# Seven block products in the last up-projection of a streaming encoder, and its start and end in column groups

## What is computed

```python
def rmsnorm(x, gain):
    return x * lax.rsqrt(jnp.mean(x * x, axis=-1, keepdims=True) + EPS) * gain

def conv_ffn(h, hist, w_up, w_conv, b_conv, w_down):      # h: (1, t, 1024), w_up: (1024, 2*2816)
    a, gate = jnp.split(h @ w_up, 2, axis=-1)
    ext = jnp.concatenate([hist, a], axis=1)
    conv = b_conv
    for j in range(3):
        conv = conv + ext[:, j:j + t] * w_conv[j]
    return (jax.nn.silu(conv) * gate) @ w_down, ext[:, t:]
...
    xp = xp + h                       # after both layers: y = rmsnorm(x, final_norm)
```

## Time and profile before

| | |
|---|---|
| median of 3 runs | 4039.38 us (4039.28 to 4047.45) |
| the profiled execution | 4032.72 us, span 4030.9 us |
| mean granted TensorE clock | 0.965 |
| TensorE, matmul, busy | 3753.4 us (93%) |
| VectorE | 2217.8 us (55%) |
| ScalarE | 1105.6 us (27%) |
| GpSimd | 647.4 us (16%) |

### The profile page before, as it was taken

How to read it: one execution, slowest core, us unless ns; L and a number is a source line. 1 busy time by engine, 2 the same in 40 slices (tenths; PEclk the granted TensorE clock), 3 DMA queues, 4 the chain that set the end, 5 groups by cost and what they waited for, 6 DMA issues and landing times. The chain is left out here.

```text
span 4030.9 us, 54343 instructions
## 1 busy us (share of the span) xinstructions
PE 3753.4 (93%) x21836; PEld 2985.1 (74%) x21836; DVE 2217.8 (55%) x4569; ACT 1105.6 (27%) x2612; POOL 647.4 (16%) x732
## 2 busy tenths in 40 slices
PE   7978899999999999999899988999899999899997
PEld 5755577777877767777677777887677777688886
DVE  1764655599954555459355553589936565421112
ACT  1123333211144442221333322111144433211111
POOL 2200220301101232030001014312000101511113
PEclk9988899999999999999999989999999999999999
DMA  4332233412212232342222113343121212332222
GB/s 148 98 93 65 75 94 101 124 52 85 91 36 78 67 97 89 91 135 77 65 77 83 40 60 118 105 119 105 56 79 41 82 38 62 127 108 80 74 73 79
DMA packets 149475, 339.53 MB, mean 84 GB/s; under 512 B 30104, under 2 KB 64472, under 8 KB 135912
## 3 DMA queue, kind: packets, MB, share of 16 engines
q1 hardware_dynamic: 89448, 291.04, 23.1%
q10 hardware_dynamic: 59776, 45.02, 3.9%
HBM read 299.33 MB, written 36.68 MB: 83 GB/s over the span
## 5 line engine op out<-in xcount | busy, mean ns | idle before, releaser
L731 PE MATMUL PS<-xn,wring 128*128 128x272 f32 (+1 forms) x8448 | 1979.0, 394 | 69.7 <-ACT dense L1032 27.7
L731 PEld LDWEIGHTS PS<-xn,wring 128*128 128x128 f32 x8448 | 1626.4, 194 | 374.9 <-issue 43.3
L731 PE MATMUL PS<-dense,wring 128*128 128x256 f32 (+1 forms) x2816 | 669.8, 397 | 17.3 <-DVE dense L1301 6.8
L1589 POOL TENSOR_TENSOR xT<-xT,res 128x272 f32<-128x272 f32 (+1 forms) x320 | 253.7, 794 | 2617.7 <-ACT res L1001 2577.7
L731 PEld LDWEIGHTS PS<-dense,wring 128*128 128x128 f32 x2816 | 543.2, 196 | 118.8 <-issue 13.0
L1369 DVE MAX8 top<-scr 128x8 f32<-128x384 f32 (+6 forms) x418 | 367.5, 879 | 12.5
L1370 DVE MATCH_REPLACE8 scr<-top,scr 128x384 f32<-128x384 f32 (+6 forms) x418 | 359.9, 861 | 0.0
L1001 ACT ACTIVATE res<-PS 128x272 f32<-128x272 f32 (+1 forms) x320 | 123.7, 389 | 604.5 <-PE PS L731 580.7
L739 PE MATMUL PS<-wring,xn 128*128 128x256 f32 (+1 forms) x1152 | 266.5, 391 | 3.2 <-ACT dense L1015 3.2
L739 PEld LDWEIGHTS PS<-wring,xn 128*128 128x128 f32 (+1 forms) x1152 | 212.7, 187 | 50.0 <-issue 6.3
L731 PE MATMUL PS<-catT,wring 128*128 128x272 f32 (+1 forms) x1024 | 234.6, 391 | 6.0 <-DMA wring<-in_wo 5.5
(11 more groups left out here) (167 smaller groups left out, 3388.8 us busy)
## 6 DMA issues: line engine op xcount, KB each, us to landing
wring<-in_wu SPq DMA_DIRECT2D x88, 1024.0 KB, 4.9
wring<-in_wf SPq DMA_DIRECT2D x88, 512.0 KB, 3.8
wring<-in_wo SPq DMA_DIRECT2D x64, 512.0 KB, 3.7
wring<-in_wd SPq DMA_DIRECT2D x96, 320.0 KB, 2.9
wring<-in_wd SPq DMA_DIRECT2D x64, 384.0 KB, 3.1
wring<-in_wn SPq DMA_DIRECT2D x16, 1024.0 KB, 5.5
kv<-out_projT ACTq DMA_DIRECT2D x48, 256.0 KB, 3.6
out_projT<-dense SPq DMA_DIRECT2D x40, 272.0 KB
```

What stands on the lines that cost most here:

```text
L731: mm = nc.tensor.matmul(PS[:, dbank(t.g0), 0:cw], wtile(t.q, i), rhs, start=(kk == a), stop=(kk == b - 1))
L1589: nc.gpsimd.tensor_tensor(x, x, res[:, i % NRES, 0:cw], ALU.add).then_inc(s_res, 1)
```

## The change

**Seven products.** For tiles 1 to 20 of F11 the four sums (two branches by two column groups) of eight blocks each become seven products of four blocks each, after Strassen and Winograd. The weights of a tile are the four blocks A11, A12 (branch a, first and second half of the 1024 inputs), A21, A22 (gate), each 128x512; the inputs are B11, B12 (first half of the inputs, column groups 0 and 1), B21, B22. GpSimd makes S3, S1, S2, S4 from the weights of the next tile (four subtractions or sums of 128x512), S1 in place of A21, the others in `kv`, which the mixers no longer use. VectorE makes T1 to T4 (128x1024 each) once, in `scr`. The products are evicted one by one (128x256), and VectorE adds them up in seven sums into a and g, before the convolution and after it. The tanh of a tile is moved behind the second eviction of the next, the product behind its fourth turn. The factor 0.5 of the gate moves into the product.

**The start and end in groups.** The input is loaded for group 0 first, the first weight tile, then group 1. The norm is split in three: `nsq`, `nsr` (root, reciprocal), `nsc` (scaling). Half 1's squares and roots of the input move from the start of P01 to before section c of P00. The stage Y0 goes: the second group's final norm of half 0 comes after two turns of F11's wo, its store (a `y` turn, j = 1) after five, and SyncE issues a store two turns after its `y` turn. The first group is stored by itself near the end of dn. The very last group is stored in four pieces. In F11 the squares are summed in `heads` instead of `xn`, and each wait of GpSimd's adds for a scaling is for its own half alone.

```diff
+SEVEN = {(1, 1): range(1, NF - 1)}
+PRODUCTS = (Product("P1", "A11", "B11"), Product("P2", "A12", "B21"), Product("P6", "S2", "T2"), Product("P5", "S1", "T1"),
+            Product("P7", "S3", "T3"), Product("P3", "S4", "B22"), Product("P4", "A22", "T4"))
+S_ORDER, T_ORDER = ("S3", "S1", "S2", "S4"), ("T3", "T2", "T4", "T1")
...
 def _project(l, h):
-    if l == 0:
+    if l == 0 and h == 0:
         _norm(l, h, 0, 0, 1)
+    elif l == 0:
+        _turn("nsc", l, h, 0, 1, 0, ng=0)
...
+        if (l, h, g) == (0, 0, "c"):
+            for j in range(2):
+                _root(0, 1, 0, j, 1)
...
             if (n, j) == (2, 1):
                 _norm(*norm, 0)
+            if (n, j) == (6, 1) and norm[0] == L:
+                _turn("y", L, h, j=0, ng=0)
+            if (kind, l, h, j) == ("wo", 1, 1, 0) and n == 1:
+                _norm(L, 0, 2, 1)
+            if (kind, l, h, j) == ("wo", 1, 1, 0) and n == 4:
+                _turn("y", L, 0, j=1, ng=0)
...
-            if n >= (0, 8, 14, 19)[p]:
+            if n >= (0, 8, 14, 19)[p] and n in SEVEN.get((l, h), ()):
+                for i in range(len(PRODUCTS)):
+                    _turn("s", l, h, n, i, load=("u", l, h, n, 0))
+            elif n >= (0, 8, 14, 19)[p]:
...
 # SyncE
-                sp.eng.dma_start(xT[:, k, 0:W[0]], io["xT"][k * P:(k + 1) * P, 0:W[0]]).then_inc(s_x[0][k], 16)
+                sp.eng.dma_start(xT[:, k, 0:GMAX], io["xT"][k * P:(k + 1) * P, 0:GMAX]).then_inc(s_x[0][k], 16)
...
+                    if nextq == 0:
+                        for kk in range(KD):
+                            sp.eng.dma_start(xT[:, kk, GMAX:W[0]], ...).then_inc(s_x[0][kk], 16)
...
-                if t.kind == "y":
-                    sp.wait_ge(s_xn, KD * (norm_of(k) + 1))
-                    out = io["yT"].rearrange("(k p) t -> p k t", p=P)[:, :, C0[t.h]:C0[t.h] + W[t.h]]
-                    sp.eng.dma_start(out, xn[:, :, 0:W[t.h]]).then_inc(s_y, 16)
+                if k >= 2 and TURNS[k - 2].kind == "y":
+                    store_y(k - 2, KD)
...
+            store_y(len(TURNS) - 1, 2)
...
 # TensorE
+                elif t.kind == "s":
+                    weights_in(pe, t.q)
...
+                    if x.s in S_ORDER:
+                        pe.wait_ge(s_ws, 4 * U + S_ORDER.index(x.s) + 1)
+                    if x.t in T_ORDER:
+                        pe.wait_ge(s_xs, 4 * list(SEVEN).index((t.l, t.h)) + T_ORDER.index(x.t) + 1)
+                    bank_free(pe, t.g0)
+                    ws, xs, cw = w_block(t, x.s), x_block(t.h, x.t), GRP[t.h][0][1]
+                    for i in range(4):
+                        mm = nc.tensor.matmul(PS[:, dbank(t.g0), 0:cw], ws[:, P * i:P * i + P], xs[:, i, :], ...)
...
 # ScalarE
-                if pending is not None:
+                if pending is not None and k > UP_END[pending[0:3]] + (2 if t.kind == "s" else TURNS[UP_END[pending[0:3]]].kind == "s"):
...
+                    dst = {"P1": part_of(t, 0), "P2": a[:, 2 + c0:2 + c0 + cw], "P6": part_of(t, 1), "P5": g[:, c1:c1 + cw],
+                           "P7": part_of(t, 2), "P3": a[:, 2 + c1:2 + c1 + cw], "P4": g[:, c0:c0 + cw]}[PRODUCTS[t.p].name]
+                    nc.scalar.activation(dst, PS[:, dbank(t.g0), 0:cw], ACT.Copy).then_inc(s_ea, 1)
...
 # VectorE
-                if pending is not None and (t.kind == "dn" or k >= LAST[("g",) + pending[0:3] + (0,)] + 2):
+                if pending is not None and (t.kind == "dn" or k >= UP_END[pending[0:3]] + (4 if t.kind == "s" else 2)):
...
+                    if name == "P6":
+                        nc.vector.tensor_tensor(u2, u2, p1, ALU.add).then_inc(s_fix, 1)
+                        nc.vector.tensor_tensor(a0, a0, p1, ALU.add).then_inc(s_fix, 1)
+                    elif name == "P7":
+                        dve.wait_ge(s_fix, fixed + 1)
+                        nc.vector.tensor_tensor(u3, u3, u2, ALU.add).then_inc(s_fix, 1)
+                    elif name == "P3":
+                        nc.vector.tensor_tensor(a1, a1, g1, ALU.add).then_inc(s_fix, 1)
+                        dve.wait_ge(s_fix, fixed + 4)
+                        nc.vector.tensor_tensor(a1, a1, u2, ALU.add).then_inc(s_fix, 1)
+                    elif name == "P4":
+                        dve.wait_ge(s_fix, fixed + 4)
+                        nc.vector.tensor_tensor(g0, g0, u3, ALU.add).then_inc(s_fix, 1)
+                        nc.vector.tensor_tensor(g1, g1, u3, ALU.add).then_inc(s_fix, 1)
...
 # GpSimd
+                if t.q + 1 in BLOCK_Q and k == FIRST_OF[t.q]:
...
+                    if B >= 2:
+                        pool.wait_ge(s_mm, TURNS[UP_END[BLOCKS[B - 2]]].g0 + 1)
+                    for i, (out, x, y, op) in enumerate((("S3", "A11", "A21", ALU.subtract), ("S1", "A21", "A22", ALU.add),
+                                                         ("S2", "S1", "A11", ALU.subtract), ("S4", "A12", "S2", ALU.subtract))):
+                        pool.wait_ge(s_ws, 4 * B + i)
+                        nc.gpsimd.tensor_tensor(w(out), w(x), w(y), op).then_inc(s_ws, 1)
```

More of the change, by code:

```diff
@@ L153 @@
 NG = TURNS[-1].g0 + TURNS[-1].ng
+UP_END = {(t.l, t.h, t.n): k for k, t in enumerate(TURNS) if t.kind in ("a", "g", "s")}
+BLOCKS = [(l, h, n) for l, h in PROJS if (l, h) in SEVEN for n in SEVEN[l, h]]
+BLOCK_Q = {}
+for _t in TURNS:
+    if _t.kind == "s":
+        BLOCK_Q[_t.q] = BLOCKS.index((_t.l, _t.h, _t.n))
+FIRST_OF = {}
+for _k in range(len(TURNS) - 1, -1, -1):
+    if TURNS[_k].q >= 0:
+        FIRST_OF[TURNS[_k].q] = _k
 TILE_DONE = [max(t.g0 + t.ng for t in TURNS if t.q == q) for q in range(len(TILES))]
+SCALES = [k for k, t in enumerate(TURNS) if t.kind == "nsc"]
 NORMS = [k for k, t in enumerate(TURNS) if t.kind == "nsq"]
-PROJS = [(0, 0), (0, 1), (1, 0), (1, 1)]
 LAST = {(t.kind, t.l, t.h, t.n, t.p): k for k, t in enumerate(TURNS)}
@@ L397 @@
 LEAD = 22
-_first, _last = turns_of("P00", "P01"), turns_of("P11", "F10", "Y0")
+_first, _last = turns_of("P00", "P01"), turns_of("P11", "F10")
 STEPS = [(kind, m) for m in range(4) for kind in "XBCM"]
@@ L656, in store_rows, with store_y @@
                 sp.eng.dma_start(projN[l, r0:r0 + u.w, p * CW:(p + 1) * CW], tout[:u.w, i % NTO, :]).then_inc(s_to[i % NTO], 16)
+            def store_y(k, step):
+                t = TURNS[k]
+                c, cw = GRP[t.h][t.j]
+                for kk in range(0, KD, step):
+                    sp.wait_ge(s_xn, KD * norm_of(k) + kk + step)
+                    out = io["yT"][kk * P:(kk + step) * P, xcols(t.h, c, cw)].rearrange("(k p) t -> p k t", p=P)
+                    sp.eng.dma_start(out, xn[:, kk:kk + step, c:c + cw]).then_inc(s_y, 16)
             nextq = 0
@@ L710, in dense_tensor @@
                         pe.wait_ge(s_acc, norms_before(k) - 4 + 1)
-                        mm = nc.tensor.matmul(out, mean[:], xn[:, SUM, c:c + cw], start=True, stop=True)
+                        mm = nc.tensor.matmul(out, mean[:], squares_of(t)[0], start=True, stop=True)
                     mm.then_inc(s_mm, 1)
@@ new lines, in dense_vector @@
+                if t.kind == "s":
+                    (c0, cw), (c1, _) = GRP[t.h]
+                    a, g, fixed = ab[:, t.n % 2, :], gb[:, t.n % 2, :], len(PRODUCTS) * BLOCKS.index((t.l, t.h, t.n))
+                    a0, a1, g0, g1 = a[:, 2 + c0:2 + c0 + cw], a[:, 2 + c1:2 + c1 + cw], g[:, c0:c0 + cw], g[:, c1:c1 + cw]
+                    p1, u2, u3 = (part_of(t, i) for i in range(3))
+                    name = PRODUCTS[t.p].name
+                    if name in ("P6", "P7", "P3", "P4"):
+                        dve.wait_ge(s_ea, t.g0 + 1)
+                    if name == "P6":
[12 more added lines that the diff above has]
+                        nc.vector.tensor_tensor(g1, g1, u3, ALU.add).then_inc(s_fix, 1)
```

126 lines of the change are left out of this document (103 added, 23 removed).

## The result

The changed kernel takes 4009.4 us (median, 4004.9 to 4015.0) against 4041.6 us for the kernel before on the same chip: ratio 0.9929, 95% interval 0.9916 to 0.9941. It is faster, but by about 30 us where the forecast was 52, and 4009.4 lies just above the predicted range of 3968 to 4008. The profiled execution has a span of 4003.0 us, 27.9 less than before, where the sum of the prediction was 51.8.

The account below looks back on a forecast made before the run. TensorE, busy 93% of the span, was taken as the bound. The terms -34.4 + 3 - 13 - 5 + 1.5 - 3.9 = -51.8 us, taken off the median of 4039.38, gave 3987.6 us, range 3968 to 4008.

Parts of the forecast that it names:

- the joint P00 to P01: Half 1's squares, means and roots moved before section c of P00: -5 us (+2 to -10), half of 10.3.
- the weave: Mixer steps in P00, P01 and F10 shift by a turn or so, sign unknown: 0, +- 5 us.
- about 1 us each: Waits that stay for half 1's squares, means and roots at their new place before section c of P00.
- the products: F11, tiles 1 to 20: 28 matmuls instead of 32, 1.72 us less a tile, -34.4 us if TensorE stays the bound.
- four held VectorE instructions a tile: F11 tiles: each of four GpSimd sums holds one VectorE instruction by up to 1.13 us, 4.5 us, costing nothing.
- F10 to F11: Waits of 5.85 and 5.48 us go as norm and store move: -13 us (-8 to -16).
- the 2 us for catT: F10 to F11: wo can't start before VectorE's last step on catT ends, so 2 us of waiting stay.
- the end: Last piece of the store of y is 256 KB instead of 2048 KB: -3.9 us (-3 to -4.5).
- the collision at n = 0: F11: GpSimd's S sums meet VectorE's scaling of the second column group, four instructions held: +3 us (0 to +4).
- The start: Eight more load issues ahead of the last constant: +1.5 us (0 if bytes bound it, 4 if issue does).
- The pair of VectorE and GpSimd as the bound: Rival, F11: a tile takes 12.5 to 13.4 us, 9 to 27 us of gain lost, 3997 to 4015; chance 0.12.
- The joints keep their waits: Rival: F10 to F11 gains only 5.5, P00 to P01 nothing, the start costs 4: 4003 us; chance 0.16.

Follow-up runs that it names:

- the places kept: The changed kernel with all 596 mixer steps between the same matmul groups as in the kernel before (also "places put back"): 3983.4 us, ratio 0.9863.
- P00's and P01's places put back: The changed kernel with only the mixer steps of P00 and P01 at the places of the kernel before: 3993.5 us, ratio 0.9887.

## Why the prediction was wrong

**The step that failed** is the one that sized the joint P00 to P01 and the weave together: "-5 (+2 to -10)" and "0, +- 5". I noted that the mixers' steps shift by a turn or so and took the shift as a small error of unknown sign, without working out the new order. It was worth -12.0 with the places kept and +9.7 as the change made it, and in F00 to F10 another +6.3 against -0.3: 28 us between the two orders by the offsets, 26 by the medians. Some of the 28 are the clock (5.7 of the 21.7 in P00 and P01), which the sum had no term for. The list of turns is in the code, and so are the planner's rules; the new order could have been read off before any run, and the earlier trace rows alone could not show it.

**The mechanism** is one of queues. In P00 VectorE is the late engine (busy 37.9 of 40 us from 180 to 220 us in the kernel before), and a relu that needs it blocks ScalarE. Where the relu stands behind the squares, TensorE works on; one group earlier, TensorE waits up to 16.9 us and goes on at half its clock. My estimate of "about 1 us each" for the waits at the new place was right for the order of the kernel before (1.0 at the longest) and wrong for the one that ran.

**The joint itself** was undersized: with the places kept, the moved norm is worth 12.7 us, not 5. I halved 10.3 on the ground that mixers' waits would show instead; they did not: TensorE's idle time in P00 and P01 differs by 10.1 us between the two kernels, and the clock adds 3.0.

**Right:** the products (-34.5 for -34.4; no wait of TensorE inside the tiles behind the first, four held VectorE instructions a tile, 4.0 us for the 4.5 I had set); F10 to F11 (-13.2 for -13, with the 2 us for catT); the end (-4.7 for -3.9, just past the estimate's outer bound of -4.5). **Mis-sized:** the collision at n = 0, +4.5 for +3: six GpSimd sums instead of four fell into the scaling. In the nine kernels whose first sums stand there it is +4.5 to +7.6, though the eight scalings always take 8.58 or 8.59 us; what differs is the clock behind the short waits. From 3562 to 3580 us it is 1.00 in the changed kernel and 0.81 in the one with P00's and P01's places put back (+7.5), and the 22 records behind the last scaling took 5.01 and 7.96 us:

```profile
3571.77 5.01 PE L835 MATMUL PS<-xn,wring 128*128 128x256 f32 x22 [0.71 <-DVE xn L1454]
```

```profile
3570.60 7.96 PE L871 MATMUL PS<-xn,wring 128*128 128x256 f32 x22 [0.70 <-DVE xn L1490]
```

The start: +4.0 for +1.5, at its upper bound, as issue and not bytes bound it; but run by run it had no clear effect at the end.

**The range.** The single terms' bounds, added as the prediction gives them, reach from 3969.5 to 4009.0 us, not from 3962 to 4018. The measured 4009.4 is where they end with every term at its worst.

**The rivals.** The pair of VectorE and GpSimd as the bound came nearest in time (3997 to 4015, middle 4006) and was wrong in mechanism: TensorE stayed the bound in the tiles. "The joints keep their waits" (4003) was wrong too: F10 to F11 gained all of its 13. With the places put back the same terms sum to -53.8, and that kernel's 3983.4 lies 4 from the forecast of 3987.6; this is partly luck, as there the joint won 7 us more than its term, and the start and the collision together lost 5 us more than theirs.

The Trainium skill's rule (SBUF — State Buffer, section "SBUF: two separate sides") of an exclusive lock for a whole instruction is too strict for what these traces show: within the 8.59 us of the eight scalings at n = 0 lie five GpSimd sums of 1.26 to 1.33 us, 6.6 together, and 0.5 us of a sixth. One after the other with the 3.26 of the scalings alone they would fill 10.3.

## What to carry to other kernels

A planner that places work by counting turns changes its plan when a turn is added anywhere: print the order of before and after, compare it in units of real work, and price each pair of items that changed places, or pin the old places while one thing is tried. In front of a wait look at what stands behind it in the same queue: two steps that wait for the late engine, put ahead of independent work, made a wait of 16.9 us for TensorE and a kernel 20 us slower, over a third of what the whole change could bring. Price the clock behind a long wait with the wait itself. A small error term "sign unknown" on an order that the code already fixes is no error term but work not done.

## What the runs showed of the hardware

Beside a GpSimd sum of 512 columns one VectorE instruction with SBUF operands takes 0.89 to 1.07 us longer, not each one: 1.73 for 0.75, 1.49 for 0.42. The holding is mutual, but smaller on GpSimd's side (1.59 and 1.60 us for 1.27). Beside the same sums, eight scalings of 256 columns with a scalar operand took 8.59 us instead of 3.26, 0.89 us more for each of six sums.

TensorE's granted clock was at one of two levels, and it fell to the lower one in and behind stretches in which TensorE waited. The first eviction shows it: in the ten kernels with the split load it came 2.7 to 3.7 us late where the mean clock of the first 50 us was 1.00, 3.7 and 4.0 at 0.97, and 6.1 to 6.5 at 0.93, with the same instructions up to there.

Stages with the same instructions differed by up to 8.7 us in their offsets from one execution to another (P10 and P11 in the kernels with the places put back), mostly by the clock. With plain groups in F11 the offset to the kernel before stayed at 8.84 to 8.86 us from wo's last groups to the last eviction, but for two single evictions at 8.58: where TensorE never waits a trace repeats, and where engines hand work to each other it does not.
